# A two-block layer on one core: x brought in by feature, and the order of the first stage changed

## The reference

```
h = rms_norm(x, pre_mix_norm)        # x * rsqrt(mean(x*x) + EPS) * w
proj = einsum('bsd,dc->bsc', h, w_in)
att_q, att_k, att_v, gdn_qkv, gdn_z, gdn_a, gdn_b = split(proj)
l_own = einsum('bhqd,bhkd->bhqk', q, k) * scale + rel_bias[...]   # 8 heads of 64
qkv = silu(causal_depthwise_conv(gdn_qkv, conv_w))  # 4 taps, 1536 channels
q, k = l2_normalize(q) * dh**-0.5, l2_normalize(k)
beta = sigmoid(b); g = -exp(A_log) * softplus(a + dt_bias)
decay = exp(where(causal, g_cum[i] - g_cum[j], -inf))
m = strict(k_beta k^T * decay); uw = triangular_solve(m + eye, ...)
```

## Time and profile before

| | us |
|---|---|
| median of three runs | 912.06 |
| the profiled execution | 912.35 |
| its span in the trace | 910.5 |
| TensorE busy | 898.0 (99%) |
| weight loads of TensorE | 765.9 (84%) |
| VectorE busy | 602.7 (66%) |
| ScalarE busy | 461.4 (51%) |
| GpSimd busy | 90.9 (10%) |

### The profile page before, as it was taken

One profiled execution on the slowest core, in us unless ns is written; L12 is line 12 of the kernel. 1 busy time (PEld: TensorE's weight loads), 2 busy tenths in 40 slices (PEclk: granted clock), 3 DMA queues, 4 the chain that ended last, 5 costly groups with the idle time before them and its releaser, 6 DMA issues.

```text
span 910.5 us, 12778 instructions
## 1 busy us (share of the span) xinstructions
PE 898.0 (99%) x5466; PEld 765.9 (84%) x5466; DVE 602.7 (66%) x705; ACT 461.4 (51%) x558; POOL 90.9 (10%) x92
## 2 busy tenths in 40 slices
PE   9999999999999999999999999999999999999997
PEld 8989888888888887888888878778788888888886
DVE  6889985777666557687867565555656666564665
ACT  7765554555444446645444255453355555454443
POOL 2142100100000000000125310110100000000000
PEclk9999999999999999999999999999999999999999
DMA  8734523244555554544565534454454356445531
GB/s 325 281 108 177 174 67 117 93 162 185 188 193 198 200 199 179 220 164 161 185 231 185 185 123 188 152 185 166 163 202 163 139 177 236 175 183 223 185 139 47
DMA packets 24218, 159.81 MB, mean 176 GB/s; under 512 B 3241, under 2 KB 3769, under 8 KB 5857
## 3 DMA queue, kind: packets, MB, share of 16 engines
q1 hardware_dynamic: 21600, 152.58, 45.8%
q0 software_dynamic: 2272, 6.24, 2.0%
q10 hardware_dynamic: 288, 0.17, 0.1%
HBM read 157.91 MB, written 2.63 MB: 176 GB/s over the span
## 4 chain that ended last, share of the span: by engine, by line
PE 80%; DVE 12%; ACT 4%; issue 2%; DMA 0%; POOL 0%; POOLq 0%; DVEq 0%; ACTq 0%
PE banks L494 31%; PE banks L462 20%; PE banks L465 10%; DVE t_wl L1582 4%; PE banks L434 4%; PE banks L585 3%; PE banks L522 2%; PE banks L739 2%; PE banks L993 2%; PE banks L405 1%; ACT t_wh L1114 1%; DVE t_hold L1600 1%; DVE t_xt L1600 1%; PE banks L943 1%; PE banks L1075 1%
## 5 line engine op out<-in xcount | busy, mean ns | idle before, releaser
L1582 DVE TENSOR_TENSOR t_wl<-t_raw,t_wh 128x2048 fp32r<-128x2048 f32 x139 | 318.0, 2309 | 123.2 <-ACT t_wh L1114 121.9
L462 PE MATMUL banks<-t_hx,t_wh 128*128 128x512 f32 x992 | 312.0, 396 | 0.0
L1114 ACT CAST t_wh<-t_raw 128x2048 fp32r<-128x2048 f32 x139 | 261.5, 1906 | 12.8 <-DMA t_raw<-in_W 8.1
L465 PEld LDWEIGHTS banks<-t_hx,t_wl 128*128 128x128 f32 x992 | 186.3, 188 | 43.8
L465 PE MATMUL banks<-t_hx,t_wl 128*128 128x256 f32 x992 | 194.9, 278 | 0.0
L462 PEld LDWEIGHTS banks<-t_hx,t_wh 128*128 128x128 f32 x992 | 153.3, 189 | 2.4
L494 PE MATMUL banks<-t_wh,t_hx 128*128 128x512 f32 x320 | 102.3, 396 | 0.0
L494 PEld LDWEIGHTS banks<-t_wh,t_hx 128*128 128x128 f32 x320 | 59.5, 188 | 12.7 <-issue 0.6
L494 PE MATMUL banks<-t_wl,t_hx 128*128 128x512 f32 x160 | 61.1, 390 | 0.0
L434 PE MATMUL banks<-t_hx,t_wh 128*128 128x256 f32 x336 | 60.6, 285 | 0.4 <-ACT t_hx L1157 0.4
L2187 POOL TENSOR_TENSOR t_st<-t_st,t_half 128x1 f32<-128x1 f32 (+1 forms) x18 | 10.6, 589 | 432.5 <-DVE t_st L1608 430.7
(11 more groups left out here) (310 smaller groups left out, 1265.5 us busy)
## 6 DMA issues: line engine op xcount, KB each, us to landing
t_raw<-in_W SPq DMA_DIRECT2D x143, 1024.0 KB, 4.8
skew<-scr POOLq DMA_DIRECT2D x1, 1536.0 KB, 16.3
t_x<-in_x SPq DMA_DIRECT2D x2, 512.0 KB, 4.8
t_tab<-in_tab POOLq DMA_DIRECT2D x1, 640.0 KB, 7.1
out<-t_xt SPq DMA_DIRECT2D x2, 320.0 KB, 2.3
t_raw<-in_W SPq DMA_DIRECT2D x1, 512.0 KB, 6.9
t_T<-skew POOLq DMA_DIRECT2D x4, 128.0 KB, 2.5
t_xt<-skew POOLq DMA_DIRECT2D x4, 128.0 KB, 2.4
```

The lines of the kernel that those rows point to most:

```text
L462: e.matmul(bank[b + c], M.wh[:, h, wk], M.hx[:, k, :, :].rearrange("p a s -> p (a s)"), start=k == 0, stop=False)
L465: m = e.matmul(bank[b + c][:, 0:S], M.wl[:, h, wk], M.hh[:, k, :], start=False, stop=k == 7)
L1114: e.copy(M.wh[:, h, 0:n], M.raw[:, r, 0:n]).then_inc(q.sem, q.tick(("hi", i)))
L1582: e.tensor_tensor(M.wl[:, h, 0:n], M.raw[:, r, 0:n], M.wh[:, h, 0:n].bitcast(F32), ALU.subtract).then_inc(q.sem, q.tick(("lo", i)))
```

## The change

- x is loaded a second time, by feature (`xT`, four loads of 256 KB), in turns with quarters of the first weight unit. `hh` and `hl` are made from it directly, with the norm's weights but without the norm's root; `turn_x` and the scaling of x by token are gone for this stage. Units 0 and 1 arrive and are converted in quarters, units 2 and 3 in halves. TensorE takes them piece by piece (`pieced_unit`).
- Each user of a product puts the root in: a 128x256 tile `rbc` (made by TensorE from a broadcast root, copied by ScalarE) multiplies the convolution's inputs and the attention keys, on VectorE; a root per token scales z, the values, the gates and the attention scores.
- The half unit "Z" is gone. Its 16 columns come from a small array `wab` (128 KB, scaled by GpSimd), with 8 fp32 matmuls of 32 columns of weights each in four column quarters of the array. They are added up by a matmul with a folded identity.
- The bias matmul moves into unit conv 2. Running sums move from after conv 1 to after conv 3. The decays are subtracted, cut at zero and taken to the exponential by ScalarE in the step of conv 3 (17 instructions, ahead of the SiLU of units 0 and 1); VectorE masks them in the step of conv 4.
- VectorE takes the convolution's inputs out of PSUM (`scaled`), in place of ScalarE. In its last step the taps come first, then a weight unit, then the sum of squares.
- Attention keys are computed ahead of queries, and come out on VectorE. `zw` moves on GpSimd to after the last product `Ug`.

```diff
-    u = [("Z", "w_in", 3472)]
-    u += [("B", "w_in", 256 * i) for i in range(4)]
+    u += [("B", "w_in", 256 * i) for i in (2, 3, 0, 1)]
...
+            def pieced_unit(tile, by, name, mid=None):
+                order = [(p, n, k, c) for p in range(PIECES[i]) for n in range(3)
+                         for k in range(p * per, p * per + per) for c in range(2)]
+                for n_, (p, n, k, c) in enumerate(order):
+                    q.wait_ge(*((DV, ("lo", i, p)) if n == 2 else (AC, ("hi", i, p))))
+                    q.wait_ge(*((DV, ("xl", "in", k)) if n == 1 else (AC, ("xh", "in", k))))
...
             for u in range(6):                                  # TensorE
+                if u == 0:
+                    gates_unit()
+                elif u == 1:
+                    gates()
+                    roots()
-                if u == 1:
+                elif u == 3:
                     b = take("sums")
...
             for u in range(6):                                  # ScalarE
-                next_unit()
+                if u != 4:
+                    next_unit()
...
-                q.wait_ge(PE, ("conv", u))
-                e.copy(M.cin[:, 2 * u:2 * u + 2, 3:], halves(bank[at["conv", u]][:])).then_inc(
-                q.wait_ge(q, ("cin", u))
+                q.wait_ge(DV, ("cin", u))
...
-                if u == 1:
+                if u == 3:
                     q.wait_ge(DV, "gc")
                     e.activation(M.eg, M.gcum, ACT.Exp).then_inc(q.sem, q.tick("eg"))
                     q.wait_ge(DV, "kdx0")
                     e.activation(M.kdx, M.kdx, ACT.Exp).then_inc(q.sem, q.tick("kdx"))
-                elif u:
-                    if u == 2:
-                        silu_of(0)
-                    silu_of(u - 1)
-                    if u == 5:
-                        silu_of(5)
+                    next_unit()
+                    for g in range(4):
+                        b = at["decay", g]
+                        q.wait_ge(PE, ("decay", g))
+                        for i in range(4):
+                            s = 4 * g + i
+                            e.activation(M.dU[:, s, :], bank[b][:, i * 128:i * 128 + 128], ACT.Relu, scale=-1.0,
+                                         bias=M.gcum[:, s:s + 1]).then_inc(q.sem, q.tick(("drop", g)))
+                    q.wait_ge(q, ("drop", 3))
+                    e.activation(M.dU[:], M.dU[:], ACT.Exp, scale=-1.0).then_inc(q.sem, q.tick("dexp"))
+                    silu_of(0)
+                    silu_of(1)
+                elif u == 4:
+                    silu_of(2)
+                    silu_of(3)
+                elif u == 5:
+                    silu_of(4)
+                    silu_of(5)
...
             for u in range(6):                                  # VectorE
-                next_unit()
+                if u:
+                    scaled(u)
+                if u < 5:
+                    next_unit()
...
+                for k in range(1, 4):                            # the taps
...
+                if u == 3:
+                    q.wait_ge(PE, "sums")
...
+                elif u == 4:
+                    q.wait_ge(AC, "dexp")
+                    tt(M.dU[:], M.dU[:], rep(M.triu, 16), ALU.mult, "dU")
                 elif u == 5:
+                    next_unit()
                     for c in range(2):
                         for w in range(2):
                             q.wait_ge(AC, ("sq", w, c))
...
+            keys(0)
+            q.wait_ge(q, "dU")
             tt(M.AT, M.dU[:], rep(M.nstrict, 16), ALU.mult, "dS")
             next_unit()
             next_unit()
+            keys(1)
...
-                tt(P, bank[at["S", h]][:, 0:384], M.Ts[h % 4], ALU.add, ("P", h))
+                for i, (l, r) in enumerate(parts):
+                    stt(P[:, l:r], bank[at["S", h]][:, l:r], M.ms[:, i:i + 1], M.Ts[h % 4][:, l:r], ALU.mult, ALU.add,
...
+            for p in range(4):                                   # SyncE
+                a = slice(p * 2 * S, p * 2 * S + 2 * S)
+                e.dma_start(M.xT[:, a], A["xT"][:, a]).then_inc(LD[f"xT{p}"], 16)
+                piece(0, p)
+            e.dma_start(M.wab, A["wab"]).then_inc(LD["wab"], 16)
+            for p in range(4):
+                piece(1, p)
             for t in range(2):
                 e.dma_start(M.x[:, t, :], A["x"][t * 128:t * 128 + 128, :]).then_inc(LD[f"x{t}"], 16)
```

More of the change, by code:

```diff
@@ L93, in plan @@
 def plan():
[L94 to L95 removed]
+    u = [("B", "w_in", 1536 + 256 * i) for i in range(6)]
     u += [("C", "w_in", 3072, k) for k in (0, 4)]
[L97 removed]
+    u += [("B", "w_in", 256 * i) for i in (2, 3, 0, 1)]
     u += [("C", "w_in", 1024, k) for k in (0, 4)]
@@ L278, in memory @@
         M.kd = tm[:, 0, 0:512]
-        M.triu, M.nstrict, M.ones, M.near, M.same, delta, M.cap = (tab[:, i, :] for i in range(7))
+        M.triu, M.nstrict, M.ones, M.near, M.same, delta, _ = (tab[:, i, :] for i in range(7))
         M.delta = delta[:, 0:BASE]
@@ L414, in b_unit @@
                 opened(b)
[L416 to L422, removed]
-                for n_, (c, k, n) in enumerate(order):
[L424 to L428, removed]
-                    w, a = ((0, 0), (0, 1), (1, 0))[n]
-                    if halved:
-                        first, last = n_ == 0, n_ == len(order) - 1
-                    else:
-                        first, last = k == 0 and n == 0, k == 7 and n == 2
-                    m = e.matmul(bank[b][:, c * S:c * S + S],
-                                 W[w][:, h, k * 128 * nt + c * 128:k * 128 * nt + c * 128 + 128],
-                                 H[a][:, k, :], start=first, stop=last, skip_group_check=halved)
-                    if n_ == len(order) - 1:
-                        m.then_inc(q.sem, q.tick(tile, ("unit", i)))
@@ L439, in b_unit @@
+                order = [(c, k, n) for c in range(2) for k in range(8) for n in range(3)]
+                for n_, (c, k, n) in enumerate(order):
+                    w, a = ((0, 0), (0, 1), (1, 0))[n]
+                    m = e.matmul(bank[b][:, c * S:c * S + S], W[w][:, h, k * 256 + c * 128:k * 256 + c * 128 + 128],
+                                 H[a][:, k, :], start=k == 0 and n == 0, stop=k == 7 and n == 2)
                     if mid and n_ == 23:
                         mid()
+                m.then_inc(q.sem, q.tick(tile, ("unit", i)))
@@ L610, in gates @@
                 q.wait_ge(AC, "ab")
-                transpose(bank[b][:, 0:128], M.ab[:, 0:128])
-                transpose(bank[b][:, 128:256], M.ab[:, 128:256]).then_inc(q.sem, q.tick("gates"))
+                q.wait_ge(DV, "fold")
+                for c in range(2):
+                    m = e.matmul(bank[b][:, c * 16:c * 16 + 16], M.ab[:, c * 128:c * 128 + 128], M.fold, start=True,
+                                 stop=True)
+                m.then_inc(q.sem, q.tick("gates"))
                 drain(b, DV, "eb")
@@ L2240, in gpsimd @@
                 load_T(h)
+            q.wait_ge(DV, ("Ug", 2, 1))
+            for c in range(2):
+                z = heads(M.zz[:, c, :])
+                q.wait_ge(AC, ("zz", c))
+                q.wait_dma(LD["small"])
+                tt(z, z, rep(par("gdn_w"), 8), ALU.mult, ("zw", c))
             for by in (PE, AC, DV):
```

332 lines of the change are left out of this document (184 added, 148 removed).

## The result

The changed kernel takes **922.45 us** (median of 4 runs, 922.04 to 923.39) against 912.11 beside it: 1.0115 times the kernel before, 95% interval 1.0100 to 1.0130. The sign of the forecast is right, its size is not: +10.3 us instead of +3.7, outside the range of 907.5 to 920. The profiled execution took 923.39, its span is 921.6 against 910.5.

The account below looks back on a forecast made before the run. TensorE, nearly gapless, and the ScalarE/VectorE chain arrive together, so lengthening the latter stalls at full price. 3.3 (queries) + 0.2 (scores) + 0.2 (clock) = +3.7 on 912.35: 916.0, by median 915.8; range 907.5 to 920.

Parts of the forecast that it names:

- first stall: Middle of conv 5: TensorE reaches the transposes at 42.5 and waits nearly 10 us for ScalarE's SiLU, until 52.3.
- A: Rival: the lead of 8.9 us is kept, conv 5 ends 8.5 earlier; -6.4, 905.7 us; chance 0.15.
- B: Rival: VectorE keeps up, `gc` at 36, everything behind 3.5 earlier; about -0.1, 912.0 us; chance 0.23 together with D.
- D: Rival: the moved root is off the path, queries 4 us earlier, B's time; chance 0.23 together with B.
- C: Rival: clock stays low through conv 5 (+2.7), or gate matmuls run serially: 917.5 to 918.5, both 920; chance 0.20.
- ScalarE to the SiLU: Step of conv 3: ScalarE's work behind `gc`, through exponentials, subtractions and SiLUs, takes 12.5 us, to 52.3.
- The start: Loads and splitting piece by piece at 380 to 426 GB/s; decays reached at 29.9 + 0.35 against 39.13, lead 8.9 us.
- Conv 0: First convolution: VectorE's splittings end at 9.7, four matmuls remain, conv 0 ends at 10.25 us.
- what is hidden: Work off the path: norm and scaling beside conv 0 and 1, bias row, `zw`; only scores in two instructions cost +0.2.
- The root: GpSimd's root between sum of squares and scalings takes 5.62 us, to 71.1, while VectorE converts unit 8.
- The clock: TensorE's clock falls in the first stall; conv 5 taken 1.7 late, 0.2 of it at the end; +2.9 if it stays low.
- second stall: Queries' transposes: TensorE arrives at 75.0 and waits 3.7 us for VectorE's queries, ready near 78.7; old spacing from there.

Follow-up runs that it names:

- e1: Changed kernel with ScalarE's SiLUs 0 to 3 ahead of the wait for the decays' sums, gate exponentials behind z's SiLU: 918.28 us (1.0065).
- e2: Changed kernel with VectorE's sum of squares and root scalings ahead of unit 5's taps instead of behind: 917.98 us (1.0065).
- e8: Changed kernel with both reorderings, e1 and e2, together: 915.06 us (1.0033).
- e4: Changed kernel with x by feature in two loads instead of four, and units 0 and 1 in halves: 925.91 us (1.0149).
- e5: Changed kernel with mean squares from x by feature (wrong results), x by token loaded behind unit 3: 922.55 us (1.0117).
- e6: Changed kernel with VectorE waiting for GpSimd's root and scaling the keys before converting its next weight unit: 927.26 us (1.0166).
- e9: Changed kernel plus one unused VectorE instruction, about 0.35 us, between the scaled sums and the next unit's conversion: 919.87 us (1.0084).
- e3: Changed kernel plus 30 and 12 TensorE matmuls of constants ahead of the transposes at the two stalls: 920.40 us (1.0095).
- e11: Changed kernel with e1, e9's spacer, ScalarE's unit conversion before the Relus, its unit 5 tap earlier, VectorE's unit 7 before unit 5's taps: 913.10 us (1.0011).
- e16: e11 plus queries before conversion, mask later, decays' sums inside conv 3 and copied earlier, root split keys first, GpSimd's v by beta behind queries: 908.57 us (0.9964).

## Why the forecast was right in kind and wrong in size

- **The mechanism.** Both stalls came where the forecast put them, for the engines it named, 7.6 us for "nearly 10" and 3.4 for 3.7, with the clock at half behind the first; the later trace is nearly a moved copy. e1 shortens the first stall and e2 removes the second, and rivals A, B and D are out, as are both halves of C: the clock was full again within conv 5, the gates ran in parallel.
- **ScalarE to the SiLU: right.** 12.5 forecast, 44.80 to 57.39 measured, 12.6. VectorE's 21.1 from unit 2 to the sums: 21.1, from 23.7 to 44.77. Gates in four quarters: 1.07 for 1.0.
- **The start: the step that failed.** "Unit 2 lands [...] its halves at 15.3 and 16.6" became 18.5 and 21.36; "VectorE is through at 18.7" became 23.7. I had taken the best microseconds of the earlier trace rows, 380 to 426 GB/s, for the rate of the whole start; the changed kernel moved 250 GB/s in its first 12 us (before: 304), 3.0 MB where the forecast's pace has 3.65. By my estimate that is 1.6 of the 4.8 us.
- **What else made unit 2 late.** I had let the transfers arrive one after the other. Up to the end of unit 2 SyncE asks for 5.5 MB (x twice, three units, the small arrays), and when that half landed its queue had moved 6.75 MB. The other 1.2 MB belong to units 3 and 4, which were asked for behind it; at the 411 GB/s of 12 to 24 they are 3.0 us. No run holds units 3 and 4 back, so this split stays an estimate.
- **Conv 0.** "Conv 0 ends at 10.25" became 14.6: the pieces came later, and ScalarE's table load of 1.28, which the kernel before has at 1.65 us ahead of x, now stands behind x at 4.04. TensorE's clock was also at 0.57 from 8 to 12, but it is not the cause: it was 1.00 there in e1 and e8, and conv 0 ended at 15.2 and 14.4.
- **What the late start cost.** The first stall hid none of it, since VectorE's chain sets its end: +4.9 on the queries. e4 and e5 show that it is neither the size of the pieces nor the second x alone: weights and `rbc` are late together, and the forecast had counted the scaling under what is hidden. What keeps the rate low in the first 12 us stays open.
- **The root: mis-sized.** Forecast 5.62 with "VectorE converts unit 8" beside it, measured 7.43: +1.8. The forecast took the duration from a row of the kernel before, where no conversion was under way when the root began. e6 (5.46), e9 (5.57), e2 (5.63) settle it.
- **The clock: mis-sized.** I gave the second stall no fall of the clock ("From there the old spacing holds"), though its 3.4 us without work are more than the "nearly 3" of the earlier trace rows on which I argued for the first. 3.67 + 6.19 against 1.97 + 5.75: +2.1, and e3 brings 2.05 back. At the first stall the half rate was free, as forecast: the path there runs over ScalarE's copies until 63.5.
- **The sum again.** From the forecast's +3.7: +4.9 start, +0.5 between sums and root, +1.8 root, -0.5 the scalings (4.2 for 4.7), +2.1 clock make 12.5; at `XT` it was +12.6. 1.5 came back behind it: +11.1 in the span. Of these, 0.8 is a gap of TensorE's own at 135.9 in the kernel before, longer than the three waits that the forecast called the longest; 0.7 stays open.
- **The other check I gave myself**, 5% on the path for 3 us, was about durations. VectorE's 21.1 and ScalarE's 12.5 came within 1%; the third stretch, from the last first tap to the queries, took 21.8 us for 20.4, 7% more, with the root in it. The path's beginning was not a duration but an arrival, and it stood in no row. Two sums of the forecast are off by little: rival A's 48.8 is 36 + 12.5 = 48.5, and the terms of VectorE's 21.1 add up to 21.25.

## What to carry to other kernels

A forecast over several engines adds durations, which rows give well, to a starting moment, which they do not: bound the landing of the first loads from the mean rate of the whole start, not from its best stretch, add what is asked for right behind them, and let the range carry it. When one engine gains a lead (TensorE began the decays at 35.13 instead of 39.13) and the program's order on the others is left as it was, the lead turns into a stall; ask for each instruction that stands behind a wait whether it needs that wait. And look for the stretch in which the other engine is full: once TensorE's waits are nearly gone, as from e11 on, the time is the start of that stretch plus nearly a constant, and what moves that start counts.

## What the runs showed of the hardware

- GpSimd's root, started while VectorE is 0.17 us into a conversion of 128x2048, takes 7.43 us; started 0.17 us ahead of it, 5.57; with VectorE idle, 5.46. It behaves as if it waited for the one under way, and is hardly slowed by one that begins later; nor is that conversion (2.34 us in e9, 2.28 alone). The Trainium skill, "GPSIMD Engine Reference", its table of the engine, tells of contention with VectorE instructions that have two SBUF inputs. The trace agrees, the conversion being such a one (7.43 against 5.46), and e9 shows that the order of the two starts decides whether it is paid.
- The other way round it is a slowing: VectorE's 128x512 products with a broadcast factor take 0.65 to 0.7 us alone and 1.4 to 1.5 beside GpSimd's products (1.54 and 0.68 us for the same scaling of keys in the changed kernel). A conversion of 128x2048 keeps its 2.28 there, while the GpSimd pair takes 3.9 instead of 2.5 (e8, e16).
- TensorE had no work from 82.0 to 85.4 us. Its granted clock was 1.00 from 80 to 82, 0.78 from 82 to 84, 0.50, the 1.2 GHz level, from 84 to 88, and 1.00 again from 90 to 92. With 42 matmuls of constants in the two stalls it was 1.00 from 48 to 96 (e3).
- When the second half of unit 2 landed, at 21.36 us, SyncE's queue had moved 1.2 MB more than was asked for up to it: the transfers of one queue overlap. That the half landed later for it is my estimate above and no run's result.
